# Loading the first weights of the delta-rule gate `z` during the heads' second pass, into the ring slot that GpSimd's solves used

## What is computed

```python
def gdn_project(h, w_in, conv_w, a_log, dt_bias):
    proj = h @ w_in                                  # 1024 -> 4096 (q,k,v) + 2048 (z) + 64 (b,a)
    qkv = short_conv(proj[..., :GDN_QKV_W], conv_w)
    ...
    z = proj[..., GDN_QKV_W:GDN_QKV_W + GDN_VW].reshape(B, T, GDN_V_HEADS, GDN_DV)
    ba = proj[..., GDN_QKV_W + GDN_VW:].astype(jnp.float32).reshape(B, T, 2, 2, GDN_V_HEADS)
    beta = jax.nn.sigmoid(ba[..., 0, :])
    g = -jnp.exp(a_log) * jax.nn.softplus(ba[..., 1, :] + dt_bias)
    return q, k, v, z, beta, g
```

## Time and profile before

| what | value |
| --- | --- |
| median of 3 runs | 4293.78 us (4288.1 to 4298.75) |
| the profiled execution, its own time | 4290.65 us |
| its span in the profile | 4288.9 us |
| mean granted clock of TensorE | 0.96 of full |
| PE busy | 3906.2 us (91%) |
| DVE busy | 2527.1 us (59%) |
| the gates' products | 1428.9 to 1440.1 us |
| `gdn_prepare` starts | 1447.8 us |
| the second pass ends, SP issues the loads of z | 1930.2 us |
| z's first product starts | 1935.2 us |

### The profile page before, as it was taken

The page is one execution under the profiler, slowest core; times in us unless marked ns, Lnnn a source line. Parts: engine busy times, 40 slices in busy tenths (PEclk is TensorE's granted clock), DMA queues, the critical chain, the costliest instruction groups (busy, mean ns, idle before and its releaser), DMA issues. The chain is left out here.

```text
span 4288.9 us, 53310 instructions
## 1 busy us (share of the span) xinstructions
PE 3906.2 (91%) x19818; PEld 2823.5 (66%) x19818; DVE 2527.1 (59%) x4524; ACT 1219.9 (28%) x2542; POOL 1228.4 (29%) x1478
## 2 busy tenths in 40 slices
PE   7999899999899798889999999989999789669998
PEld 4577455555455586768778885568755456658886
DVE  7634799552488885557688856545533318823353
ACT  3155311100222485662021102138510211341112
POOL 1274299100000068820000275858000011430000
PEclk9999999999999899999999999999999899879999
DMA  4542356221111076535345544423011275782221
GB/s 168 194 119 86 120 174 190 106 106 61 49 69 50 21 220 171 116 84 178 126 155 171 168 145 140 141 71 98 20 57 56 97 256 193 238 228 100 74 91 66
DMA packets 287967, 533.15 MB, mean 124 GB/s; under 512 B 177024, under 2 KB 184064, under 8 KB 263424
## 3 DMA queue, kind: packets, MB, share of 16 engines
q1 hardware_dynamic: 216736, 344.70, 24.6%
q0 software_dynamic: 53312, 180.00, 14.1%
q10 hardware_dynamic: 17696, 5.56, 0.6%
HBM read 430.01 MB, written 100.01 MB: 124 GB/s over the span
## 5 line engine op out<-in xcount | busy, mean ns | idle before, releaser
L509 PE MATMUL P<-hu,ring 128*128 128x384 f32 (+1 forms) x2448 | 744.8, 458 | 10.0 <-DVE hu L644 4.0
L509 PEld LDWEIGHTS P<-hu,ring 128*128 128x128 f32 x2448 | 466.3, 191 | 264.1 <-issue 11.4
L755 PE MATMUL P<-area,ring 128*128 128x256 f32 (+1 forms) x1880 | 488.6, 416 | 39.3 <-PEq L481 17.6
L755 PEld LDWEIGHTS P<-area,ring 128*128 128x128 f32 x1880 | 359.0, 192 | 158.2 <-issue 54.2
L509 PE MATMUL P<-area,ring 128*128 128x256 f32 (+1 forms) x1584 | 442.9, 432 | 3.3 <-DVE area L644 2.7
L509 PEld LDWEIGHTS P<-area,ring 128*128 128x128 f32 x1584 | 301.6, 191 | 127.2 <-issue 4.7
L975 POOL TENSOR_TENSOR fold<-mod,vec 128x16 f32<-128x16 f32 (+1 forms) x5 | 1.0, 203 | 1175.7 <-SPq L954 1146.5
L755 PE MATMUL P<-area,hu 128*128 128x256 f32 (+1 forms) x1104 | 296.9, 423 | 0.2 <-DVE hu L857 0.2
L755 PEld LDWEIGHTS P<-area,hu 128*128 128x128 f32 x1104 | 209.5, 190 | 78.0 <-DVE hu L857 0.6
L2684 DVE SCALAR_TENSOR_TENSOR area<-area 128x1024 f32<-128x1024 f32 x124 | 196.7, 1586 | 18.0 <-ACT area L2760 15.8
L2427 PE MATMUL P<-hu,ring 128*128 128x256 f32 (+1 forms) x512 | 169.2, 492 | 15.6 <-PEq L954 15.2
(11 more groups left out here) (462 smaller groups left out, 7133.1 us busy)
## 6 DMA issues: line engine op xcount, KB each, us to landing
ring<-in_w_ffn_in SPq DMA_DIRECT2D x44, 1024.0 KB, 4.8
area<-in_w_mod SPq DMA_DIRECT2D x70, 512.0 KB, 3.5
ring<-s_c POOLq DMA_DIRECT2D x18, 1152.0 KB, 9.1
stat<-in_w_mod SPq DMA_DIRECT2D x40, 512.0 KB, 3.4
s_c<-area POOLq DMA_DIRECT2D x32, 576.0 KB, 3.1
ring<-in_w_ffn_out SPq DMA_DIRECT2D x24, 704.0 KB, 4.1
area<-s_b POOLq DMA_DIRECT2D x16, 1024.0 KB, 5.1
hu<-s_c POOLq DMA_DIRECT2D x14, 1152.0 KB, 9.1
```

The costliest lines, as they stand in the source:

```text
L509: last = mm(to, col(a, k), b[:, k, :], start=fresh and k == 0, stop=k == q - 1, skip_group_check=True)
L755: last = mm(to, a[:, 128 * k:128 * k + 128], b[k], start=fresh and k == 0, stop=k == q - 1, skip_group_check=True)
```

## The change

The gates' 64 columns are split into two groups of 32, loaded into the two slots one behind the other. So the gates take numbers 64 and 65, and z begins at 66: its first group now belongs into slot 0 and its second into slot 1. The first group is loaded in the second pass, in step 40 (key head 6, chunk step 4) right behind `fin_load(15)`; the second is loaded where both were before. All later products swap their slots.

```diff
     def products(self, pe):
-        c, slot = self.c, self.first % 2
-        pe.wait_ge(c.ring_ready[slot], 16 * (self.first // 2 + 1))
-        for t in range(6):
-            for k in range(KD):
-                last = c.nc.tensor.matmul(self.pba[:, t, :], c.u[:, k, 128 * t:128 * t + 128], c.ring[:, slot, 64 * k:64 * k + 64],
-                                          start=k == 0, stop=k == KD - 1)
-        last.then_inc(c.mm_done, 1)
+        c = self.c
+        for n in range(2):
+            slot = (self.first + n) % 2
+            pe.wait_ge(c.ring_ready[slot], 16 * ((self.first + n) // 2 + 1))
+            for t in range(6):
+                for k in range(KD):
+                    last = c.nc.tensor.matmul(self.pba[:, t, 32 * n:32 * n + 32], c.u[:, k, 128 * t:128 * t + 128],
+                                              c.ring[:, slot, 32 * k:32 * k + 32], start=k == 0, stop=k == KD - 1)
+            last.then_inc(c.mm_done, 1)
 
     def keep(self, act):
-        act.wait_ge(self.c.mm_done, self.first + 1)
+        act.wait_ge(self.c.mm_done, self.first + 2)
         self.c.nc.scalar.activation(self.ba[:, :, :], self.pba, ACT.Copy)
...
                 if s % 3 == 1 and hh + 2 < 16:
                     fin_load(sp, hh + 2)
+                    if hh + 2 == 15:
+                        sp.wait_ge(xw[HEADS - 1], 32)
+                        c.load_slot(sp, "gdn_z", 0, c.first["gdn_z"] % 2)
...
             sp.wait_ge(kept_o, 2 * HEADS)
-            c.prefetch(sp, "gdn_ba")
+            c.load_slot(sp, "gdn_z", 1, (c.first["gdn_z"] + 1) % 2)
             sp.wait_ge(h_back, 16)
...
-    a["w_gdn_z"], a["w_gdn_ba"] = blocks(w[:, 4096:6144], 2), blocks(w[:, 6144:], 1, 64)
+    a["w_gdn_z"], a["w_gdn_ba"] = blocks(w[:, 4096:6144], 2), blocks(w[:, 6144:], 1, 32)
```

## The result

The changed kernel takes 4316.83 us (median of 5 runs, 4313.37 to 4322.31), the kernel before 4290.06 (5 runs, 4285.9 to 4298.75). The ratio is 1.0059 with a 95% interval of [1.0044, 1.0075]; it is estimated from all runs, so it isn't exactly the quotient of the medians. That is slower by about 25 us, beyond the 0.3% and beyond the range that was forecast.

The account below looks back on a forecast made before the run. PE, busy for 3906 of 4289 us, was taken to bound the kernel. The terms 5.4 - 2.3 + 0.6 = +3.7 us on the profiled 4290.65 gave, against the median of 4293.78, a forecast of 4297.5 us, range 4288 to 4306.

Parts of the forecast that it names:

- Term 1: Gates: 96 more records at 113 ns add 10.83 us, less cover of 5.45: +5.4 us, also upper end; lower 0.
- The cover of 5.45 us: Tail of the k/v block: ACT idles 5.45 us until DVE's last convolution, hiding that much extra gates time.
- the copy before the silu: Gates' end: ACT's copy of the result (0.49 us) precedes the silu, which would start at about 1451.4 instead of 1446.04.
- the hidden second load: Gates' second load, issued at about 1429, lands 2.6 us later and is needed at 1440, so it costs nothing.
- Term 2: Exit of the second pass: PE waits for ACT's first step instead of z's DMA; -2.3 us, ends 0 and -2.7.
- Term 3: Second pass: small DMAs queued behind the early z load land late, PE waits at `blocks64(15)`; +0.6 us, ends 0 and 4.4.
- Rival 1: Gates: width sets the pace below 96 columns and they stay within their cover; sum -1.7 us, 4292.1 us; 6%.
- Rival 2: Second pass, `blocks64(15)`: the early load blocks the scan; 4.4 us there, sum +7.5, 4301.3 us; 6%, 3% beyond 0.3%.
- Rival 3: Exit of the second pass: z is there early, but something hidden holds PE at 1935; +6.0 us, 4299.8 us; 4%.
- rival 4: Later stages: the swapped slots alter them by over 12.9 us; 2% on the slower side, 3% on the faster.
- the chance of 0.05 on the slower side: Whole kernel: probability of slower by more than 0.3%, including 3% from a blocked scan and 2% from swapped slots.

Follow-up runs that it names:

- split-gates kernel: The changed kernel without the early load, both z loads issued where they were before; 4318.41 us against 4293.33 for the kernel before, ratio 1.0053.

## Why the prediction was wrong

**Term 1, the gates: +5.4 forecast, +21.1 measured.** This is the step that failed: "So below 96 columns the width doesn't set the pace; each record's weight load does", with 113 ns for each of the 192 records, and "I take that as the upper end as well". It rested on rows of 64 and 96 columns, and took over from them, unsaid, that the clock is 1.00. At 64 columns all of it is right (21.55 us for 192 records, +5.2). At 32 columns its pace is right as long as the clock is 1.00: the changed kernel has 20 records in the stretch 1430 to 1432, as many as the 64-column row has in 1449 to 1451. But the clock falls to 0.50 under way, and a record then takes about twice as long: with 4 us at 113 ns, some 35 records, the other 157 share 33.5 us, 213 ns each, as an estimate. For an upper end no count of these is needed: 192 records at half speed are 192 x 226 ns = 43.4 us, which is 43.4 - 10.83 - 5.45 = +27 for the term, and a mean granted clock of 0.96 said that the kernel has stretches below 1.00. That end should have stood in the range. Why narrow matmuls bring the clock down stays open; the runs show that the width does it, and the number doesn't. The cover of 5.45 us, the copy before the silu, the hidden second load (2.0 us to landing) were as forecast.

The lower clock costs 37.45 - 21.7 = 15.8 us, all past the cover, and that is the difference between the forecast and the measured term. Was there more in `gdn_prepare`? The clock is still low when it begins, but so it is in the kernel before: 0.50 in 1450 to 1452 there, behind the idle PE, and 0.50 in 1470 to 1472 here. So this isn't a new cost, and nothing beyond the 21.1 us could be told apart.

**Term 2, the exit: -2.3 forecast, -2.15 measured.** Right in its size and its mechanism: the bracket names ACT, `in_conds` is waited for no more. It also survives: at a load of `w_gdn_out` behind the z block (L731), the changed kernel is 23.1 us behind (2072.4 against 2049.3), and at z's first product it is 23.2. The split-gates kernel, whose bracket still names the DMA of z, has 6.01.

**Term 3, the early load: +0.6 forecast, 3.0 to 3.8 in three executions, not to be told apart in the changed kernel's own.** The mechanism was right, down to the group (`gdn_xa` at `blocks64(15)`), and the upper end of 4.4 held it. Mis-sized was the landing of the small DMAs behind the 1 MB: I had the last of them 7.4 us behind z's issue (1887.1 to 1894.5), and it came 8.8 and 8.9 behind it; a wait of 0.9 was forecast, 2.05 and 2.41 were measured. The low clock behind such a wait had no place in the term at all. In the changed kernel's execution 0.47 us were waited there, and the 1.2 that it is longer by stand beside the 1.1 of a kernel without the load, so most of them are the low clock behind the late `fin_load`, as far as two executions can show.

By the page "DMA: Bandwidth & Descriptors" of the Trainium skill (section "Queues, rings and completion order"), read as in the prediction, this term couldn't be 0; with landings of 3.7 us instead of 1.9 and waits of 2.05 to 2.60 us the traces agree.

**The rivals.** Rival 1 (narrow matmuls cheaper) falls: at 1.00 they cost the same, at 0.50 they are dearer than wide ones. Rival 2 was right in kind and too small to decide: its 4.4 is a little above the 3.0 to 3.8 that three executions show. Rival 3 falls by the exit's bracket, rival 4, as something large, by 0.9999 [0.999, 1.0009] for the swapped slots alone. The case that came was none of them; the chance of 0.05 on the slower side stood for other things.

**The sum with the measured terms** is 21.1 - 2.15 + 1.2 = +20.2 us in the profiled execution, where the 1.2 is all that lies behind `blocks32(15)`. The medians are 26.8 apart; with 3 to 4 us for the early load the sum is 22 to 23. Both lie inside the interval of the ratio, which is 19 to 32 us.

## What to carry to other kernels

Before matmuls are made narrower, look at the granted clock over their row in a kernel that already has such rows, and put the price at half speed into the range where there is none: here that was 15.8 us on a row of 21.7. If a set of weights has to be spread over two slots, halve the contraction and leave the columns whole: the same number of matmuls, the same width, 1.0001 instead of 1.0059, with the early load in both. A load that is moved ahead of its need should go behind the last small loads that somebody waits for; here 5 us later on its queue was early enough. In the rows the idea then keeps its gain (44.14 us instead of 45.93). In the time it is about as small as can be measured, and its interval touches no change: 4291.37 us against 4297.15, 0.9991 [0.9982, 1.0].

## What was unexpected in the hardware

- In this kernel, matmuls of 32 columns behind 128x128 float32 weight loads bring the granted clock from 1.00 to 0.50 after about 4 us, though the records show no idle PE: 17.15 us for 96 records where 64 columns take 10.83, and 37.45 us for 192 where 64 columns take 21.55. Half the columns take 1.6 to 1.7 times as long. Widths between 32 and 64 weren't run.
- A PE wait in the scan can cost more than its own length. Behind waits of 1.64, 1.71, 2.05, 2.41 and 2.60 us the clock was 0.50 in five executions; behind one of 2.04 us it stayed at 1.00. What decides isn't shown. From `blocks32(15)` to the last copy the kernel with the wait of 2.05 us lost 3.0, that with 2.41 lost 3.8.
- DMAs of 24 KB in line behind one of 1 MB from the same engine land in 3.7 to 4.0 us (medians) instead of about 1.9; 640 KB more raise the medians to 4.6 and 4.9, but not the last of the eight, which takes 3.8 to 4.0 us in all three kernels.
